# Attention products in a hybrid attention and convolution block: 128 columns of weights in place of 64

## The reference

```python
def one_block(args):
    qi, start = args
    z = jnp.einsum('bqhd,bkhd->bhqk', qi, k).astype(jnp.float32) * scale
    t = start + jnp.arange(QUERY_BLOCK, dtype=jnp.int32)
    mask = key_pos[None, :] < t[:, None]
    log_beta = jax.nn.log_sigmoid(z)
    log_1m_beta = jnp.where(mask, jax.nn.log_sigmoid(-z), 0.0)
    rev = lax.cumsum(log_1m_beta, axis=3, reverse=True)
    excl = jnp.concatenate([rev[..., 1:], jnp.zeros_like(rev[..., :1])], axis=-1)
    w = jnp.where(mask, jnp.exp(log_beta + excl), 0.0)
    return jnp.einsum('bhqk,bkhd->bqhd', w.astype(v.dtype), v)
```

## Time and profile before

| | us |
|---|---|
| median of 3 runs | 1233.47 (1233.45 to 1234.15) |
| profiled execution, its own time | 1233.28 |
| its span (first to last instruction) | 1231.4 |
| PE busy in it | 1191.3 (97%) |
| PE weight loads | 999.3 (81%) |
| record of one load of weights: 128 columns (L1463, mean), 64 columns (L1524, mean) | 0.188, 0.137 |
| record of one attend product (L1524), median | 0.273 |
| DVE busy | 680.0 (55%) |
| ACT busy | 422.1 (34%) |
| POOL busy | 478.5 (39%) |
| attend products (L1524), busy | 90.6, 704 records |

### The profile page before, as it was taken

One profiled execution on the slowest core, in us unless ns is written; L12 is line 12 of the kernel. 1 busy time (PEld: TensorE's weight loads), 2 busy tenths in 40 slices (PEclk: granted clock), 3 DMA queues, 4 the chain that ended last, 5 costly groups with the idle time before them and its releaser, 6 DMA issues.

```text
span 1231.4 us, 15527 instructions
## 1 busy us (share of the span) xinstructions
PE 1191.3 (97%) x6108; PEld 999.3 (81%) x6108; DVE 680.0 (55%) x733; ACT 422.1 (34%) x785; POOL 478.5 (39%) x363
## 2 busy tenths in 40 slices
PE   6999999999999999989999999999999999999996
PEld 5899889889888878877787888887878788878875
DVE  5349994985966855576334344443434343434346
ACT  5311451441453834553414141414131313132322
POOL 4112301301300002245828292929282828283721
PEclk9999999999999999999999999999999999999998
DMA  7203202202105211113121211121212121112113
GB/s 269 77 18 88 69 18 59 69 12 70 35 1 172 95 35 35 38 33 102 35 69 35 69 35 69 35 69 35 69 35 69 35 69 35 69 35 69 35 52 137
DMA packets 65334, 75.50 MB, mean 61 GB/s; under 512 B 6064, under 2 KB 54828, under 8 KB 65262
## 3 DMA queue, kind: packets, MB, share of 16 engines
q1 hardware_dynamic: 64078, 72.38, 18.9%
q10 hardware_dynamic: 1184, 2.13, 0.5%
HBM read 63.92 MB, written 6.32 MB: 57 GB/s over the span
## 4 chain that ended last, share of the span: by engine, by line
PE 74%; POOL 12%; issue 7%; ACT 2%; DVE 2%; DMA 1%; POOLq 0%; SPq 0%; ACTq 0%; DVEq 0%
PE ps L1656 18%; PE ps L1635 17%; PE ps L1463 15%; PE ps L1524 7%; PE ps L1584 5%; POOL wa_lo L586 4%; PE ps L1424 4%; PE ps L1493 3%; PE ps L1511 3%; POOL wb_lo L586 2%; POOL wa_f L607 1%; POOL wa_f L601 1%; POOL wa_f L604 1%; DMA out<-ost 1%; POOL wb_f L601 1%
## 5 line engine op out<-in xcount | busy, mean ns | idle before, releaser
L1344 DVE TENSOR_TENSOR mix<-ps,mix 128x512 f32<-128x512 f32 x176 | 121.3, 691 | 137.6 <-PE ps L1656 137.6
L1106 DVE SCALAR_TENSOR_TENSOR acc<-u_pad,par,acc 128x1024 f32<-128x1024 f32 x116 | 146.6, 1303 | 0.3
L540 POOL TENSOR_TENSOR wp_lo<-raw,wp_hi 128x1024 fp32r<-128x1024 f32 x16 | 60.7, 3796 | 213.6 <-ACT wp_hi L685 213.6
L1656 PE MATMUL ps<-wd_hi,act_hi 128*128 128x512 f32 x352 | 137.1, 389 | 1.4 <-DVE act_lo L1333 1.4
L1656 PE MATMUL ps<-wd_hi,act_lo 128*128 128x512 f32 x352 | 136.9, 389 | 0.0
L1656 PE MATMUL ps<-wd_lo,act_hi 128*128 128x512 f32 x352 | 136.9, 389 | 0.0
L586 POOL TENSOR_TENSOR wa_lo<-wa_f,wa_hi 128x512 fp32r<-128x512 f32 x58 | 79.4, 1372 | 133.0 <-ACT wa_hi L907 129.1
L1463 PE MATMUL ps<-hn_hi,wp_hi 128*128 128x348 f32 (+2 forms) x352 | 118.5, 337 | 0.0
L1463 PE MATMUL ps<-hn_lo,wp_hi 128*128 128x348 f32 (+2 forms) x352 | 117.6, 334 | 0.0
L1463 PE MATMUL ps<-hn_hi,wp_lo 128*128 128x348 f32 (+2 forms) x352 | 117.5, 334 | 0.0
L1635 PE MATMUL ps<-t_hi,wa_hi 128*128 128x512 f32 x232 | 91.9, 396 | 4.3 <-POOL wa_lo L586 3.9
(11 more groups left out here) (160 smaller groups left out, 2584.4 us busy)
## 6 DMA issues: line engine op xcount, KB each, us to landing
raw<-in_w_gate SPq DMA_DIRECT2D x11, 1024.0 KB, 5.3
raw<-in_w_up SPq DMA_DIRECT2D x11, 1024.0 KB, 5.3
wd_f<-in_w_down SPq DMA_DIRECT2D x11, 1024.0 KB, 4.9
raw<-in_w_in SPq DMA_DIRECT2D x16, 512.0 KB, 3.8
xin<-in_x SPq DMA_DIRECT2D x8, 512.0 KB, 10.8
wo_raw<-in_w_out SPq DMA_DIRECT2D x4, 1024.0 KB, 8.2
mix<-in_x SPq DMA_DIRECT2D x8, 512.0 KB, 3.5
out<-ost SPq DMA_DIRECT2D x8, 512.0 KB, 2.6
```

What stands on the lines that cost most here:

```text
L540: pool.tensor_tensor(dst, raw[:, slot, :], hi.bitcast(F32), ALU.subtract).then_inc(wlo_done, 1)
L1106: dve.scalar_tensor_tensor(out=acc[:, j % 2, :], in0=u, scalar=w, in1=acc[:, j % 2, :], op0=ALU.mult, op1=ALU.add).then_inc(conv_step, 1)
L1344: dve.tensor_tensor(hrow, ps[:, TB + n % 4, :], hrow, ALU.add).then_inc(d_added, 1)
L1656: last = pe.matmul(ps[:, TB + n % 4, :], a[s][:, t, i * P:(i + 1) * P], w_[m][:, t, dh * BANK:(dh + 1) * BANK], start=(t == 0 and s == m = ...
```

## The change

The value steps of each head stand in a new array `vs_of`, per key block and head 128 columns wide: the 64 columns of the head's own steps, and 64 columns of zeros at the place of the other head. The zeros are written once by POOL; DVE writes the steps with two instructions, one per head, of half the size each. `attend` uses all 128 columns as weights and writes all 128 partitions of the region; both heads of a query tile are summed into the same region, the zeros adding nothing to the other head's half. The start flag of a bank is set only in the first unit that writes to it. PE waits for two more zeroings at the first unit of a pair.

```diff
@@ (allocation) @@
-             ("v_last", [P, PAIRS, TILES], F32)],
+             ("v_last", [P, PAIRS, TILES], F32), ("vs_of", [P, KB, 2, P], F32)],
@@ POOL, before the first pair @@
             pool.memset(vs[:, 0, :], 0.0).then_inc(v_zeroed, 1)
             pool.memset(vs_back[:, 0, :], 0.0).then_inc(v_zeroed, 1)
+            for h in range(2):
+                pool.memset(vs_of[:, :, h, DH * (1 - h):DH * (1 - h) + DH], 0.0).then_inc(v_zeroed, 1)
             pool.memset(gq[:, :, 0:FRONT], 0.0).then_inc(front_zeroed, 1)
@@ DVE, step_values @@
                 dve.wait_ge(v_loaded, 64 * (p + 1))
-                dve.tensor_tensor(vs[:, :, :], vs_back[:, :, :], vs[:, :, :], ALU.subtract).then_inc(v_stepped, 1)
+                for h in range(2):
+                    dh = slice(DH * h, DH * h + DH)
+                    dve.tensor_tensor(vs_of[:, :, h, dh], vs_back[:, :, dh], vs[:, :, dh], ALU.subtract).then_inc(v_stepped, 1)
@@ PE, attend @@
                         pe.wait_ge(pv_evac, past(NG * p))
-                        pe.wait_ge(v_stepped, p + 1)
+                        pe.wait_ge(v_stepped, 2 * (p + 1))
+                        pe.wait_ge(v_zeroed, 4)
+                    ends = [n_ for n_, u in enumerate(UNITS) if u[1] // 4 == i // 4]
                     for b, blocks in enumerate(t_banks(i)):
                         m = CT[n] + b
                         pe.wait_ge(t_copied, past(NT * p + m + 1))
                         for j, kb in enumerate(blocks):
-                            last = pe.matmul(ps[DH * h:DH * h + DH, PV + i // 4, (i % 4) * P:(i % 4 + 1) * P],
-                                             vs[:, kb, DH * h:DH * h + DH], w_t[:, m % 4, j, :],
-                                             start=(kb == 0), stop=(kb == i + 1))
+                            last = pe.matmul(ps[:, PV + i // 4, (i % 4) * P:(i % 4 + 1) * P],
+                                             vs_of[:, kb, h, :], w_t[:, m % 4, j, :], start=(kb == 0 and n == ends[0]),
+                                             stop=(kb == i + 1 and n == ends[-1]), skip_group_check=True)
                         last.then_inc(pv_used, 1)
```

More of the change, by code:

```diff
@@ L139, in hybrid_block @@
             [("ost", [P, 2, D], F32), ("gfb", [P, D], F32)])
-        (xin, xnorm, xsq, g1b, v_stage, wv_raw, qst, kd, gq, w_t, vs, vs_back, v_last, b0_hi, b0_lo, b1_hi, b1_lo, hn2f,
+        (xin, xnorm, xsq, g1b, v_stage, wv_raw, qst, kd, gq, w_t, vs, vs_back, v_last, vs_of, b0_hi, b0_lo, b1_hi, b1_lo, hn2f,
          skip_1, act_lo, wd_hi, wd_lo, act_hi, skip_2, act_f, skip_3, wd_f) = region(
```

## The result

The changed kernel takes 1216.12 us, the median of 4 runs (1215.46 to 1216.80), against 1233.81 for the kernel before (1233.45 to 1234.20) on the same chip. The ratio is 0.9856, 95% interval 0.9843 to 0.9870: 17.7 us less, and 17.7 was forecast. The profiled execution took 1215.46 us, its span is 1213.6.

The account below looks back on a forecast made before the run. PE, busy 97% of the span, was taken to set the pace, losing time at attend borders. 20.1 - 0.7 - 0.7 - 1.0 = 17.7 us saved gave a median of 1215.8 us; forecast 1212 to 1219, 8-in-10 range 1212 to 1222.

Parts of the forecast that it names:

- The borders: PE entering and leaving attends: the change of width costs 0.10 to 0.20 us a border; removing it gains 20.1 us.
- One sign: PE at an attend's exit to scores: scores should start 0.11 us after the last attend product, in place of 0.20.
- The weight load: Attend products on PE: loading 128 columns in place of 64 adds 0.001 us a product, 0.7 us over 704.
- Rival A: Attend products on PE: the wide load hides less well, 0.120 us a product, 7.0 us in all, 1222.1; chance 0.11.
- D: Attend products on PE: the wide load doesn't run behind the preceding product, costing 77 us, total 1293; chance 0.05.
- DVE's second subtraction: DVE ahead of its split of q's second half: two instructions cost 0.18 us more a pair, on the path, 0.7 us.
- The last pair: PE waits for DVE's scans there: 0.3 us lost at step 4, 0.7 at the last unit, together 1.0 us.
- POOL: Two more zeroings of 576 columns on POOL take 1.2 us once, off the path, so cost nothing.
- ACT's third bank: ACT's copies at step 4: 0.30 us slack, 0.24 given back; just fits, otherwise 0.1 us lost four times.
- the clock: Start of the feed-forward: a stretch at the lower clock, worth 1.3 us, can go or be joined by another.
- Rival B: First three pairs: freed time turns partly into waits for ACT and DVE, 5 us more lost, 1220.8; chance 0.11.
- Rival C: Attend borders: the gap comes from the kind of work, not the width, and stays; 1234.9 us; chance 0.05.

Follow-up runs that it names:

- half: Changed kernel, but head 1's attends have 64 columns of weights again while head 0 keeps 128; 1224.63 us, ratio 0.9933.
- mask64: Changed kernel, but the bf16 mask product behind the scores has 64 columns of weights in place of 128; 1228.21 us, ratio 0.9965.
- w96: Changed kernel with 96 of the 128 columns of weights in all attends, head 1's last 32 left out; 1213.25 us, ratio 0.9846.
- two_steps: Kernel before, with only DVE's subtraction of the value steps split into two halves, written in place; 1232.20 us, ratio 1.0001.
- late: Changed kernel with both value-step subtractions moved behind DVE's split of the second half of q; 1219.18 us, ratio 0.9876.
- taps: Changed kernel with 11 convolution taps of the last pair moved into DVE's idle time ahead of it; 1215.97 us, ratio 0.9851.
- mixlast: Changed kernel with the low half of the first output tile moved behind the last scan on DVE; 1216.04 us, ratio 0.9852.

## Why the prediction was right, and where it was not

*The borders: 20.1 us, right within 4%.* The idle time of weight loads is gone, *half* returned half of the gain with exactly 32 gaps, and *mask64* put the same kind of price at a border of its own. Read one by one in the two traces, with two distances added at each side of every attend, the borders gave these means: 53 entries behind transposes and 6 behind projections 0.142 us each, 4 behind mask products 0.088, 32 exits to scores and 6 to projections 0.192, 23 exits to transposes 0.141 (the 24th ends in the last unit's wait). That is 19.3 us. The attends beside the layer norm, which the forecast left out, gave 0.3 more. One sign came out otherwise: scores start 0.03 and not 0.11 after the last attend product, though the two distances together fell as forecast. The Trainium skill's rule in "TensorEngine Tiling (Array Packing)", Key Properties, that a change of tiling mode drains TensorE, agrees with *half* and *mask64*: each side costs 0.09 us or more in start distance, and the load behind it some 0.05 more. The runs show the lost time, not that it is a drain. *w96* shows which side of the border 96 columns are on: beside 128 they run without a gap.

*The weight load: 0.7 us, too small.* The size was read from two digits of one row. The mean distances give 0.1116 - 0.1092 = 0.0024 us a product, 1.7 us over 704; 1.4 of it lies inside the attends, and the rest is in the borders as read above. *w96* gives between 1.2 by its ratio and 2.0 by its distances. Rival A, at 7.0, was far off, and so was D: the load hides nearly whole. The rule in the Trainium skill's "TensorE: Matmul & The Clock Gate", LDWEIGHTS, gives by estimate 107 ns for 128 columns, just below the product and so free; here the step from 96 to 128 columns is already seen, so the measurement decides for a small price.

*DVE's second subtraction: 0.7 us on the path, wrong in three pairs and in size.* The step that failed is "It is on the path: DVE works without a break from there to its split of the second half of q", carried from the first pair to all four. In the first pair it holds: the split follows the scan by 0.03 us, and the cost there is 0.07, not 0.18, since two subtractions take 1.41 us and not the 1.52 worked out from the splits of q. In the second and third pair the split starts by PE's last product of q and then ACT's copy; DVE was idle 0.11 us ahead of it before and 0.04 after in the second, so the cost is 0 and there was little to spare. In the last it is 0.05. *two_steps* left the distance from mark to mark as it was, and *late* took the subtractions away and left PE's 0.76 us.

*The last pair: 1.0 us, too large.* The two places were the right ones: 0.26 at step 4 (0.3 forecast; *taps* gives it back) and 0.37 at the last unit (0.7 forecast; *mixlast* gives it back). The latter was sized as if the whole gain of two attends met a fixed time, and ACT and DVE came along with part of it. Together 0.63.

*POOL, ACT's third bank and the clock.* POOL has two more instructions in the same chain share of 12%. In the first three pairs no wait of PE on `w_t` appeared; the slack of 0.30 us shrank to 0.06 and did fit. The clock's stretch stayed. Rival B is out. A pair's borders give 5.0 us and its loads take 0.35, and the distances from mark to mark fell by 4.58, 4.65 and 4.55, so next to nothing turned into waits. Rival C is out by *half* and *mask64*.

So the sum, 20.1 - 0.7 - 0.7 - 1.0 = 17.7, reads as measured 19.3 + 0.3 - 1.4 - 0.1 - 0.6 = 17.5; the layer norm's start moved by 17.45 and the medians by 17.7. That the total came out so close is luck: the borders were taken 0.8 too large with 0.3 beside them left out and the loads 0.7 too small, 1.2 us too optimistic, while the DVE term was 0.6 and the last pair 0.4 too large, 1.0 us too pessimistic. The mechanism, its places and the size of its main term are shown.

What stays open: where between 64 and 96 columns the border appears, and whether the 0.0025 us come from the load's length or from the partitions written. No other width and no other moving length was tried.

## What to carry to other kernels

Where PE is busy 97% and yet is to be made faster, read distances from start to start at the borders between kinds of work, and hold the widths in the records (128*64, 128*128) against each other: here 0.09 to 0.19 us a border were hidden in records that look busy. Where the length of the products changes at the border too, add the next distance to the first. If the narrow products stand alone among wide ones, a zero half in the weights can cost less (0.0025 us a product, 0.03 for a group of 11) than the two borders (19.6 / 64 = 0.31 us a group); a kernel with long narrow streams has less to gain. An added instruction on an engine that works without a break is only a loss if the next one that others wait for starts by this engine and not by another. Look up what that one starts by, in every pair and not in one, before it is put in the sum.

## What the runs showed of the hardware that was not expected

Float32 weights of 96 columns (record 128*96) run beside products of 128 without a gap; weights of 64 don't, in float32 (*half*) or in bf16 (*mask64*). The price of a border is much the same for both types and kinds of work: mask to transpose 0.17 against 0.07 us with bf16, transposes to attend 0.20 against 0.11 with float32. And an attend product of 128 columns of float32 data starts 0.109 us after the last one where the loads have 64 or 96 columns, and 0.112 where they have 128; transposes, whose loads have 128 columns but a shorter record (0.141 in place of 0.192), stay at 0.109. Loads that fit behind their product by an estimate of their length can still show in the third digit, and over 704 products in the microseconds.
